# Two-layer hybrid decoder trunk: mixers placed between projection tiles, and retention's rotation moved to VectorE

## The chip, the cores and the metric

One core of one Trainium2 chip runs the whole program. The time is device microseconds of one execution, the median of three runs of the kernel before. All arithmetic is fp32. The engines are named as in the profile: PE is TensorE, DVE is VectorE, ACT is ScalarE, POOL is GpSimd and SP is SyncE, which here issues most transfers.

## What is computed

Two layers (DEPTH = 2) over 544 rows: 512 prompt positions and 8 samples of 4 new positions. D is 1024; every head has 64 channels, and there are 4 heads in retention and 4 in attention. Per layer:

```
h = x @ w_in        # 11 blocks of 256 columns: ret q,k,v,gate | dil q,k,v | conv in (2) | sgu u,v (2)
q_r, k_r = rotary(rq, rk, 64, 1e4);  ro, state = retention(q_r, k_r, rv, s0)     # chunks of 128
y_ret = layer_norm(ro) * silu(rg)
q_b, k_b = rotary(sq, sk, first 16 of 64 dims, 5e5)
y_swa = dilated_attention(q_b, k_b, sv, cached k, cached v)   # (128,1), (512,4), (2048,16), softmax combined
y_conv = silu(layer_norm(causal_depthwise_conv31(val * sigmoid(gate))))
u, v = gelu(sgu_in);  y_sgu = u * (lower_triangular(W) @ layer_norm(v) + b)
x = layer_norm(alpha * x + concat(y_ret, y_swa, y_conv, y_sgu) @ w_out)
x = layer_norm(alpha * x + moe(x))   # 4 groups, best group, best 2 of its 8 SwiGLU experts, 32 experts in all
```

The new states, keys, values and conv rows are outputs too. Each expert has three matrices of 2 MB.

## The kernel before

The kernel is written by hand, one instruction stream per engine. The order of every stream is the order of the code; engines meet through counted semaphores: `E.need(name, n)` waits, `E.done(ins, name)` counts. `E.link` makes an engine wait for its own last result. All of it is `trunk_program`.

A layer goes like this. TensorE turns x (five row tiles: four of 128 rows and one of the 32 sample rows) into `xT`. Then come the projections in chunks: a chunk is one block of 256 columns, whose weights (1 MB) SyncE loads into one of three ring buffers, times the five tiles. `chunk` issues a chunk's tiles; ScalarE's `proj_out` empties each from PSUM into `h` with the activation that belongs to the block. Blocks stand in the order VAL, GATE (conv input), U, V (sgu), RG, RQ, RK, RV (retention), SQ, SK, SV (attention). PSUM has eight banks; projection tiles go round five of them.

While chunks run, the other engines work on blocks that are out. GpSimd multiplies VAL by GATE ("glu"); VectorE normalises V (`group_norm`), copies the conv context and runs 62 taps over 784 columns (L1099 to L1113, two halves of the channels); GpSimd rotates RQ and RK ("rot_r") and SQ and SK ("rot_s") with `rotate`, four small operations per row tile and two large ones per block. In layer 0 GpSimd also issues 22 stores that clear the experts' scratch rows, ahead of "glu".

After the last chunk nothing wide is left: TensorE turns q and k of retention and of attention (`qk_tr`, eight groups), runs retention over four chunks (`ret_scores`, `ret_products`, L650 to L667), the sample's retention, and then attention. Attention is 16 units (4 row tiles times 4 heads). Unit u has scores (`att_scores`), VectorE's mask, maximum and negation (`attend`), ScalarE's exponential, the transposed probabilities (L787), their copy, the values (`att_values`) and VectorE's scaled rows (`att_rows`). The samples' cached keys and values, 16 transfers of 640 KB through four buffers, are taken between units in pairs (`cached_key_scores`, `sample_values`). GpSimd works on retention's norm meanwhile. Then the four mixers' results are turned (`turn_rows` over `mix`), four output chunks follow, x1 is normalised and stored, and the router makes tables of which expert serves which rows: a long chain of small VectorE operations, for which TensorE waits three times.

The experts run in turns over three lanes. SyncE reloads a lane's w1 and w3 as soon as the lane's product has been made, and w2 after the second product. The first three experts are loaded while the output projection runs.

```
                for t in range(TILES):
                    E.need("x1", t + 1)
...
                def load_hidden(q, turn):
                    row, new = item_at(q, turn)
                    sp.wait_ge(sem(f"h_ps{q}"), sp.snap(lo + turn))
```

## Time and profile before

| | |
|---|---|
| median of 3 runs | 1935.23 us (1932.53 to 1937.45) |
| the profiled execution | 1938.98 us |
| its span, first to last instruction | 1936.9 us |
| TensorE busy | 1472.9 us (76%) |
| VectorE, ScalarE, GpSimd busy | 544.6, 208.8, 398.8 us |
| mean granted TensorE clock | 0.854 |
| transfers | 532.60 MB, 275 GB/s on the mean |

The granted clock is the share of full speed that TensorE was given; it has two levels here, 0.5 and 1.0, and a number between them is a mean over both. The busy time of TensorE counts instructions in flight and so says little of how near to its peak the engine works. In the tables of stretches each row is one stretch of time in us from the span's start. In the timeline an f32 matmul of the code is two records, so a 128-row tile of a chunk (eight matmuls) is x16.

### The profile page before, as it was taken

How to read it: one execution, taken by the hardware profiler on the slowest of the kernel's cores; microseconds unless marked ns; L12 is line 12 of the kernel's file. 1: busy time of each engine (PE TensorE's matmuls, PEld its weight loads, DVE VectorE, ACT ScalarE, POOL GpSimd, SP SyncE). 2: the span in 40 equal slices, each digit the busy share in tenths (PEclk: the TensorE clock that was granted, in tenths of full speed). 3: DMA queues.
4: the chain of work that ended last, by engine and by line, in shares of the span. 5: the costliest groups of instructions: out<-in, count | busy, mean ns of one | idle time of the engine just before them, and what ended most of it. 6: DMA issues, size and time to landing. Idle time of an engine off the chain costs nothing. (4 is left out here: it accounts for less than half of the span.)

```text
span 1936.9 us, 40042 instructions
## 1 busy us (share of the span) xinstructions
PE 1472.9 (76%) x16276; PEld 1012.2 (52%) x16276; DVE 544.6 (28%) x1215; ACT 208.8 (11%) x579; POOL 398.8 (21%) x533
## 2 busy tenths in 40 slices
PE   8998899949567576767499988995766758566990
PEld 7887647835334333434488874684433424333550
DVE  0395352541000000000609735236100101000116
ACT  2111030001000000000121112201000000000010
POOL 3149230111001011100311943001211101110113
PEclk9999589969788888879699977896878878887995
DMA  8711041949999999999531102265899999999824
GB/s 341 280 66 58 1 159 64 364 173 359 428 425 382 425 426 425 384 425 386 194 135 66 44 36 109 92 256 225 333 427 425 380 427 424 426 425 425 349 89 142
DMA packets 77409, 532.60 MB, mean 275 GB/s; under 512 B 14430, under 2 KB 31770, under 8 KB 48538
## 3 DMA queue, kind: packets, MB, share of 16 engines
q1 hardware_dynamic: 45466, 482.00, 60.4%
q0 software_dynamic: 11136, 35.40, 5.0%
q10 hardware_dynamic: 20736, 14.18, 2.3%
q8 instruction: 53, 0.87, 0.2%
q14 instruction: 18, 0.15, 0.0%
HBM read 772.37 MB, written 35.98 MB: 417 GB/s over the span
## 5 line engine op out<-in xcount | busy, mean ns | idle before, releaser
L871 PE MATMUL ps<-arena,xT 128*32 128x256 f32 x6912 | 477.8, 437 | 252.1 <-DMA arena<-in_w 250.5
L871 PEld LDWEIGHTS ps<-arena,xT 128*32 128x32 f32 x6912 | 274.9, 126 | 444.7 <-issue 352.9
L542 PE MATMUL ps<-arena,xT 128*128 128x256 f32 x1920 | 424.9, 382 | 0.9 <-issue 0.9
L542 PEld LDWEIGHTS ps<-arena,xT 128*128 128x128 f32 x1920 | 363.9, 191 | 51.5 <-issue 1.0
L1496 DVE COPY xT<-ps 128x128 f32<-128x128 f32 x108 | 31.5, 291 | 907.2 <-PE ps L880 907.2
L889 PE MATMUL ps<-arena,xT 128*32 128x256 f32 x3456 | 212.2, 386 | 34.0 <-DVE xT L1496 22.4
L1674 POOL COPY xT<-xT 128x1 int32 x108 | 19.7, 182 | 805.8 <-PE ps L861 805.8
L889 PEld LDWEIGHTS ps<-arena,xT 128*32 128x32 f32 x3456 | 108.7, 110 | 110.2 <-issue 27.2
L1676 POOL DMA_INDIRECT xT<-x1d,xT x108 | 105.0, 972 | 53.1 <-POOL xT L1674 49.6
L1106 DVE SCALAR_TENSOR_TENSOR arena<-arena 128x784 f32<-128x784 f32 x120 | 113.7, 1029 | 0.0
L1017 ACT ACTIVATE xT<-ps 128x128 f32<-128x128 f32 x108 | 30.0, 278 | 668.7 <-PE ps L871 668.7
L1593 POOL TENSOR_TENSOR arena<-arena,const 128x128 f32<-128x128 f32 (+1 forms) x40 | 68.8, 1719 | 73.9 <-ACT arena L956 73.6
L1022 ACT COPY xT<-ps 128x256 f32<-128x256 f32 x108 | 40.2, 373 | 293.2 <-PE ps L889 289.6
L519 PE MATMUL ps<-const,arena 128*128 128x128 f32 (+1 forms) x240 | 37.8, 311 | 43.0 <-DVE arena L1283 32.8
L953 ACT ACTIVATE arena<-ps 128x256 f32<-128x256 f32 x88 | 33.8, 384 | 273.9 <-PE ps L542 273.9
L519 PEld LDWEIGHTS ps<-const,arena 128*128 128x128 f32 (+1 forms) x240 | 30.5, 167 | 49.6 <-DVE arena L1283 34.4
L1658 POOL TENSOR_TENSOR mv<-mv,halfc 128x1 f32<-128x1 f32 (+1 forms) x10 | 13.3, 1329 | 204.9 <-DVE mv L1307 204.9
L1492 DVE COPY xT<-ps 128x256 f32<-128x256 f32 x114 | 48.4, 425 | 24.5 <-PE ps L861 24.5
L861 PE MATMUL ps<-const,xT 128*128 128x128 f32 x228 | 44.4, 277 | 10.6 <-DMA xT<-x1d,xT 9.5
L940 ACT COPY xT<-ps 128x512 f32<-128x512 f32 (+1 forms) x50 | 24.8, 523 | 189.6 <-PE ps L519 189.4
L1060 DVE TENSOR_REDUCE pstat<-arena 128x20 f32<-128x1280 f32 (+1 forms) x4 | 5.9, 1486 | 124.1 <-ACT arena L956 124.1
L880 PEld LDWEIGHTS ps<-const,xT 128*128 128x128 f32 x108 | 14.9, 138 | 44.5 <-issue 44.5
(244 smaller groups left out, 1223.1 us busy)
## 6 DMA issues: line engine op xcount, KB each, us to landing
arena<-in_w SPq DMA_DIRECT2D x324, 2048.0 KB
arena<-in_w_proj SPq DMA_DIRECT2D x30, 1024.0 KB, 5.0
arena<-in_kv SPq DMA_DIRECT2D x32, 640.0 KB, 5.1
yd<-xT ACTq DMA_DIRECT2D x432, 32.0 KB
yd<-arena POOLq DMA_DIRECT2D x22, 512.0 KB, 18.6
rowpar<-in_rowpar SPq DMA_DIRECT2D x2, 2708.0 KB, 17.2
x1d<-arena SPq DMA_DIRECT2D x8, 512.0 KB, 14.6
arena<-x1d SPq DMA_DIRECT2D x8, 512.0 KB, 6.7
```

The costliest lines, as they stand in the source:

```text
L519: ins = pe.transpose(ps[g][:, j * 128:j * 128 + n], source(t, 4 * g + j), ident[0:n, 0:n])
L542: ins = pe.matmul(bank[0:n, 0:CW], xT[:, k, 128 * t:128 * t + n], ring[slot(c)][:, k, :], start=(k == 0), stop=(k == KT - 1))
L861: ins = pe.transpose(TOKENS[:, b * 128:(b + 1) * 128], xg[q][:, b * 128:(b + 1) * 128], ident)
L871: ins = pe.matmul(HB[q][r, 0:256], xgT[q][:, k % 2, BLK * (k // 2):BLK * (k // 2 + 1)], w13[q][:, :, k, 128 * j:128 * (j + 1)], start=(k = ...
L889: ins = pe.matmul(YB[q][r, 0:256], hT[q][:, BLK * c:BLK * (c + 1)], w2[q][:, c, 256 * t:256 * (t + 1)], start=(c == 0), stop=(c == 3), til ...
L953: ins = act.activation(h[0:n, c, t, :], bank[0:n, 0:CW], func.get(c, ACT.Copy))
L1022: act.copy(yo[q], YB[q][:, 0:256]).then_inc(sem(f"y_out{q}"), 1)
L1106: ins = dve.scalar_tensor_tensor(out=acc[:, cb, :], in0=src, scalar=cw[:, cb * TAPS + j:cb * TAPS + j + 1], in1=acc[:, cb, :], op0=ALU.mul ...
L1492: dve.tensor_copy(xgT[q], TOKENS[:, 0:256].rearrange("p (b m) -> p b m", b=2)).then_inc(sem(f"xgT{q}"), 1)
L1496: dve.tensor_copy(hT[q], HIDDEN[:, 0:128]).then_inc(sem(f"hT{q}"), 1)
L1593: pool.tensor_tensor(t1[:, t], a[:, t], sb_, ALU.mult)
L1676: pool.indirect_dma_start(out=xg[q], out_offset=None, in_=x1q, in_offset=bass.IndirectOffsetOnAxis(ap=gidx[q], axis=0))\
```

## The change

The blocks are projected in another order: VAL, GATE, SQ, SK, SV, RQ, RK, V, RV, U, RG. Attention starts as soon as SQ, SK and SV are out, and its units stand between the tiles of RQ, RK and V; retention's chunks stand between those of RV and U; the mixers' results are turned between the tiles of RG. The projection now goes round two PSUM banks, ps[2] and ps[3], so that a tile waits for the tile two before it to be emptied; the other banks are the mixers'.

Work changes engines. GpSimd no longer rotates. VectorE rotates SQ and SK behind tap 26, and RQ and RK between attention's units 10 and 11 and 12 and 13, with six operations per block. The taps are cut: 38 ahead of attention, 24 between units 0 to 8 (`TAPS_AT`). VectorE also takes k's decay and retention's norm from GpSimd. ScalarE takes the building of QB (the samples' queries, eight small copies) from GpSimd and the conv rows' copies from VectorE. V's GELU is made in one operation after its chunk. GpSimd keeps the powers, the expanded values and the products of "glu".

Turned q and k no longer lie in `xT` but where x is (`sT`, `rT`, and the fourth kv buffer too). So x is loaded again before the output projection, in layer 1 from a copy in memory (`x2d`) that SyncE stores at the start of the layer. The ring has two buffers after the first three chunks. Caches are used four at a time. In the router, `run_idle` issues matmuls whose result nobody reads, where TensorE waits for VectorE.

```diff
-VAL, GATE, U, V, RG, RQ, RK, RV, SQ, SK, SV = range(NCH)
+VAL, GATE, SQ, SK, SV, RQ, RK, V, RV, U, RG = range(NCH)
+TAPS_AT = (38, 41, 44, 47, 50, 53, 54, 57, 59, 62)
...
+                if L:
+                    for t in range(TILES):
+                        sp.wait_ge(sem("x2"), (L - 1) * TILES + t + 1)
+                        sp.dma_start(x2d[128 * t:128 * t + ROWS[t], :], x[0:ROWS[t], t, :]).then_inc(sem("x_saved"), 16)
...
+                ring_load(7)
+                for i in range(2 * NKV, 3 * NKV):
+                    kv_load(i)
+                ring_load(8)
+                for i in range(3 * NKV, 4 * NKV):
+                    kv_load(i)
+                ring_load(9)
+                ring_load(10)
...
+                def tile(c, t):
+                    if t == 0:
+                        pe.wait_ge(sem(f"ring{slot(c)}"), filled(c, L))
+                    j = serial(c, t, True)
+                    if j >= 2:
+                        E.need("proj_out", j - 1)
+                    E.done(weigh(ps[2 + j % 2], c, t), "proj")
...
+                E.need("s_act", 4)
+                E.need("proj_out", (SV + 1) * TILES)
+                att_scores(0)
+                for u in range(16):
+                    if u < 15:
+                        att_scores(u + 1)
+                    if u > 10:
+                        E.need("conv_out", u - 10)
+                    if u:
+                        tile(RQ + (u - 1) // TILES, (u - 1) % TILES)
+                    if 10 <= u < 15:
+                        turn_conv(u - 10, RQ * TILES + u - 1)
+                    att_turn(u)
+                    if u:
+                        att_values(u - 1)
+                    if u == 1:
+                        new_key_scores()
+                        cached_key_scores(range(0, NKV))
+                    if u == 3:
+                        cached_key_scores(range(NKV, NB))
...
+                for n in range(4):
+                    E.need("ret_a", n + 1)
+                    if n < 3:
+                        ret_scores(n + 1)
+                    if n:
+                        E.need("ret_upd", n)
+                    ret_products(n)
+                    ret_rows(n)
+                    tile((RV, RV, U, U)[n], (3, 4, 0, 1)[n])
...
+                for t in range(2, TILES):
+                    turn_mix(t - 2)
+                    tile(RG, t)
...
+                    for k in range(n):
+                        pe.matmul(HIDDEN[:, 0:256], ident, ones2, start=True, stop=True)
...
+                    dve.tensor_tensor(t1, a, si, ALU.mult)
+                    dve.tensor_tensor(t2, b, si, ALU.mult)
+                    dve.tensor_tensor(a, a, co, ALU.mult)
+                    E.link(dve.tensor_tensor(b, b, co, ALU.mult))
+                    dve.tensor_tensor(a, a, t2, ALU.subtract)
+                    return dve.tensor_tensor(b, b, t1, ALU.add)
...
+                    if u < 9:
+                        taps(TAPS_AT[u], TAPS_AT[u + 1])
```

TensorE in the midst of attention, before: the end of unit 3 and unit 4, whose scores, transposes and values follow each other directly (L703 scores, L787 transposes, L731 cached keys, L770 values).

```order
L703 MATMUL ps<-xT 128x256 [waits att_m]
L787 MATMUL ps<-const,arena 128x128 [waits att_pT,att_p]
L787 MATMUL ps<-const,arena 128x128
L731 MATMUL ps<-arena 32x512 [waits kv1,kv0]
L731 MATMUL ps<-arena 32x512
L731 MATMUL ps<-arena 32x128 x2
L731 MATMUL ps<-arena 32x512 x2
L731 MATMUL ps<-arena 32x128 x2
L770 MATMUL ps<-arena 128x64 [waits att_y,att_pT]
```

The same place now (L642 scores, L556 a projection tile, L652 transposes, L660 values):

```order
L642 MATMUL ps<-arena 128x256 [waits att_m]
L556 MATMUL ps<-arena,xT 128x256 [waits proj_out]
L556 MATMUL ps<-arena,xT 128x256 x7
L652 MATMUL ps<-const,arena 128x128 [waits att_y,att_pT,att_p]
L652 MATMUL ps<-const,arena 128x128
L660 MATMUL ps<-arena 128x64 [waits att_pT]
```

A tile of eight wide matmuls now stands between a unit's scores and its transposes, with a wait for ScalarE's emptying of its bank; the wait for VectorE's rows (att_y) moved from the values to the transposes.

VectorE in one unit, before (L1226 inverse, L1205 to L1208 mask, maximum and negation, L1232 rows):

```order
L1226 RECIPROCAL small<-small 128x1 [waits att_p]
L1205 SCALAR_TENSOR_TENSOR arena<-ps,const 128x256 [waits att_t,att_s,dve_chain]
L1207 TENSOR_REDUCE small<-arena 128x1 [waits dve_chain]
L1208 TENSOR_SCALAR small<-small 128x1 [waits dve_chain]
L1232 TENSOR_SCALAR arena<-ps,small 128x64 [waits att_o]
```

And now, with taps (L1231) ahead of the rows (L1283):

```order
L1278 RECIPROCAL small<-small 128x1 [waits att_p]
L1271 SCALAR_TENSOR_TENSOR arena<-ps,const 128x256 [waits att_t,att_s,dve_chain]
L1273 TENSOR_REDUCE small<-arena 128x1 [waits dve_chain]
L1274 TENSOR_SCALAR small<-small 128x1 [waits dve_chain]
L1231 SCALAR_TENSOR_TENSOR arena<-arena 128x784 x2
L1231 SCALAR_TENSOR_TENSOR arena<-arena 128x784 [waits dve_chain]
L1283 TENSOR_SCALAR arena<-ps,small 128x64 [waits att_o,dve_chain]
```

Three taps stand in the unit between the negated maximum and the rows of the unit before.

TensorE in the router, now (L914 to L916 counts and places, L923 onehot products, L929 which; L908 is `run_idle`):

```order
L908 MATMUL ps<-const 128x256 x18
L914 MATMUL ps<-xT,const 128x32 [waits member]
L915 MATMUL ps<-xT,const 128x160
L916 MATMUL ps<-xT,const 128x160
L908 MATMUL ps<-const 128x256 x28
L923 MATMUL ps<-xT 128x120 [waits onehot]
L923 MATMUL ps<-xT 128x120 x9
L908 MATMUL ps<-const 128x256 x4
L929 MATMUL ps<-const,xT 1x40 [waits which]
```

The three groups of L908 are new and wait for nothing; the others stand as before.

## Rows read from the trace of the kernel before

**Rows 1.** Table of stretches: TensorE, weight loads, VectorE, ScalarE, GpSimd; clock, transfers
```profile
5.00:187.00 182.00, 177.85 (x1484) 153.26 (x1484) 90.31 (x113) 35.57 (x98) 85.33 (x106) 1.00 0.48 183
187.00:236.00 49.00, 42.49 (x272) 32.27 (x272) 13.39 (x42) 6.34 (x13) 11.51 (x29) 0.60 0.10 36
236.00:302.00 66.00, 58.13 (x328) 31.77 (x326) 32.12 (x94) 18.85 (x53) 16.30 (x6) 0.83 0.41 147
...
414.00:426.00 12.00, 7.63 (x77) 4.23 (x75) 2.61 (x11) 1.28 (x1) 4.17 (x5) 0.68 0.15 46
...
428.00:850.00 422.00, 293.07 (x4267) 166.28 (x4259) 36.96 (x132) 27.95 (x86) 52.54 (x91) 0.85 0.98 407
```

**Rows 2.** TensorE's timeline, projection: start, length, line, tiles [idle before <-releaser]
```profile
73.35 14.08 PE L542 MATMUL ps<-arena,xT 128*128 128x256 f32 x64
87.36 1.10 PE L547 MATMUL ps<-arena,xT 128*32 128x64 f32 x64
...
90.14 14.08 PE L542 MATMUL ps<-arena,xT 128*128 128x256 f32 x64
...
310.54 14.05 PE L542 MATMUL ps<-arena,xT 128*128 128x256 f32 x64 [0.43 <-issue]
```

**Rows 3.** TensorE's timeline, attention's units 4 and 13 with cached keys and values
```profile
246.20 2.35 PE L731 MATMUL ps<-arena 128*32 128x512 f32 x16
...
248.84 0.70 PE L703 MATMUL ps<-xT 64*128 64x256 f32 x2
...
286.44 1.12 PE L703 MATMUL ps<-xT 64*128 64x512 f32 x2
287.49 0.66 PE L787 MATMUL ps<-const,arena 128*128 128x128 f32 x4
288.08 2.35 PE L758 MATMUL ps<-arena 128*32 128x256 f32 x20
290.36 0.62 PE L760 MATMUL ps<-arena 32*32 32x256 f32 x4
290.91 1.10 PE L770 MATMUL ps<-arena 128*128 128x64 f32 x8
```

**Rows 4.** TensorE's timeline, retention's rows stage
```profile
207.56 0.69 PE L657 MATMUL ps<-arena 128*128 128x64 f32 x2
```

**Rows 5.** GpSimd's timeline: glu, the rotation's first operation, the building of QB
```profile
49.83 2.88 POOL L1573 TENSOR_TENSOR arena<-arena 128x1280 f32<-128x1280 f32 x1
...
121.40 27.75 POOL L1593 TENSOR_TENSOR arena<-arena,const 128x128 f32<-128x128 f32 x1 [36.75 <-ACT arena L956]
...
204.36 1.97 POOL L1638 COPY arena<-xT 64x16 f32<-64x16 f32 x8
```

**Rows 6.** VectorE's timeline: a pass of V's norm, the taps
```profile
76.26 1.49 DVE L1062 TENSOR_TENSOR arena<-arena,pstat 128x1280 f32<-128x1280 f32 x1
...
92.00 56.83 DVE L1106 SCALAR_TENSOR_TENSOR arena<-arena 128x784 f32<-128x784 f32 x60
```

**Rows 7.** ScalarE's timeline: its first table load and what follows
```profile
6.21 1.28 ACT L940 ACT_TABLE_LOAD   x1 [6.21 <-PE ps L519]
7.50 1.07 ACT L940 COPY xT<-ps 128x512 f32<-128x512 f32 x2
```

**Rows 8.** Table of stretches of 4 us, columns as in rows 1
```profile
200.00:204.00 4.00, 3.77 (x18) 3.55 (x18) 0.90 (x4) 0.00 (x0) 3.92 (x5) 0.50 0.00 0
...
264.00:268.00 4.00, 2.31 (x11) 1.44 (x9) 3.72 (x14) 2.12 (x6) 3.92 (x2) 0.59 0.12 50
276.00:280.00 4.00, 4.00 (x25) 1.81 (x27) 1.53 (x3) 1.29 (x3) 0.00 (x0) 0.70 0.00 0
```

**Rows 9.** TensorE's timeline, router (onehot products) and the first two experts' products
```profile
410.26 4.62 PE L843 MATMUL ps<-xT 128*128 128x120 f32 x20 [9.89 <-DVE xT L1459]
...
420.31 6.04 PE L871 MATMUL ps<-arena,xT 128*32 128x256 f32 x64 [1.05 <-DVE xT L1492]
...
427.61 3.66 PE L871 MATMUL ps<-arena,xT 128*32 128x256 f32 x64
```

More of the change, by code:

```diff
@@ L564, in _ @@
+                tile(SQ, 0)
+                tile(SQ, 1)
                 E.need("glu", 1)
@@ new lines, in _, with ret_scores @@
+                E.need("smp_rows", 1)
+                E.need("smp_y", 1)
+                turn_pair(RQ, RK, "r_tr", lambda k: (("r_act", "r_dve")[k % 2], k // 2 + 1))
+                tile(RV, 1)
+                def ret_scores(n):
+                    for hd in range(NH):
+                        hp, hh = hd // 2, hd % 2
+                        ins = pe.matmul(ps[4 + hh][:, hp * 128:(hp + 1) * 128], rT[half(hh), 2 + hp, n * 128:(n + 1) * 128],
+                                        rT[half(hh), hp, n * 128:(n + 1) * 128], start=True, stop=True)
+                    E.done(ins, "ret_s")
@@ new lines, in _ @@
+                E.need("vexp", 1)
+                for hd in range(NH):
+                    hp, hh = hd // 2, hd % 2
+                    ins = pe.matmul(ps[4 + hp][half(hh), :], h[0:NS, RK, 4, hd * HD:(hd + 1) * HD],
+                                    vexp[:, hd, :, :].rearrange("p b e -> p (b e)"), start=True, stop=True)
+                E.done(ins, "smp_o")
+                tile(U, 3)
+                tile(U, 4)
+                E.need("sgu_vn", 1)
+                E.need("sgu_w", 1)
+                wT = CP("sgu_wT").rearrange("p (g t) -> p g t", g=4)
@@ L1098, in _, with taps @@
                 cw, cbias = CP("conv_w"), CP("conv_b")
-                for j in range(TAPS):
-                    for cb in range(2):
+                def taps(first, last):
+                    for k in range(first, last):
+                        j, cb = k // 2, k % 2
                         src = ctxb[:, cb, j:j + ACCW]
@@ new lines, in _ @@
+                for hp in range(2):
+                    ins = dve.scalar_tensor_tensor(out=s0[:, hp, :], in0=s0[:, hp, :], scalar=C("c_decay_s")[:, hp:hp + 1],
+                                                   in1=ps[4 + hp][:, :], op0=ALU.mult, op1=ALU.add)
+                E.done(ins, "smp_upd")
+                centre(last, NH, HD, last_stat)
+                spread(last, NH, HD, last_stat)
+                E.link(along(sv, RP("sgu_ln_g"), ALU.mult))
+                E.done(along(sv, RP("sgu_ln_b"), ALU.add), "sgu_vn")
```

992 lines of the change are left out of this document (508 added, 484 removed).

## The prediction, made before the changed kernel ran

> **What bounds the kernel now.** I read the table of stretches first, since the page's shares average over unlike stages. It shows a layer in four pieces [rows 1]. In 5 to 187 TensorE is busy 177.85 of 182 us: eleven projection chunks. In 187 to 302 (retention, then attention) it counts as busy for 100 of 115 us, but at a granted clock of 0.60 and 0.83. Then come the transposes of the mixers' results, and from 310.5 the output projection [rows 2]. From 428 on the transfers of expert weights keep their engines 0.98 busy: that piece is as long as its bytes, and only its start can move. So the path to the start of a layer's weight stream is TensorE's own order, and the question is how long TensorE needs for it when light and wide work are mixed. VectorE is busy 90.31 + 13.39 + 32.12 us in 5 to 302 [rows 1]; it is not the bound. Layer 1 repeats all this.
>
> The timeline gives the units. A chunk is 14.01 us for four 128-row tiles (3.50 each) and 1.03 for the 32-row tile [rows 2]. At full clock, each from its start to the next row's: a score takes 0.63 us with 256 keys and 1.05 with 512, so 0.41 and 0.84 (estimated) with 128 and 384; turning the probabilities 0.2 to 0.59 and values 0.27 to 1.04 by keys, of which the last are shown; a pair of caches 2.28, and with values 0.55 more [rows 3]. Of retention the trace has only the lower clock: 0.62 us per pair of records in its rows stage [rows 4].
>
> **The change part by part.** First the path of layer 0 up to the first output-projection tile, now at 310.5.
>
> (a) Five chunks, x's transposes and the conv context are there as before: 90.1 us [rows 2]. New: the context transposes now come after chunk 2's second tile (50.4), but GpSimd has the gate's product only at 52.7, because it clears the experts' scratch rows first [rows 5]: +2.4, in layer 0 alone (no clearing in layer 1). Then attention's q and k are turned here, paced by four ScalarE copies of 0.54 [rows 7] with some 0.1 of handoff each: +3.9. The rotation that gates them is VectorE's now, 12 operations of 160 elements at some 0.33, behind tap 26 of 62. Taps start at 55 and take 0.947 each [rows 6], so 26 end at 79, when k's chunk is out, and the rotation ends at 83, before TensorE asks (85): no wait. Sum 96.4.
>
> (b) Start of attention. The first score waits for ScalarE to empty chunk SV (1.1 us, estimated), and the first exponential for eight small copies that now build QB on ScalarE (1.97 on GpSimd [rows 5], taken 2.2), a table load of 1.28 that stands ahead of the wait, and itself, about 0.6. From the last SV tile to the first turned probabilities: 5.2 us, in which TensorE works 0.8. A table load's end is followed by a copy at once: it starts at 6.21, and the copy at 7.50 [rows 7]. The page ScalarE: Activation LUTs of the Trainium skill (section What ACT_TABLE_LOAD costs) gives 2.66 us per switch, a drain included. By that the sum would be 1.4 us worse here in each layer; that row doesn't agree with it.
>
> (c) The attention loop, 16 units with 15 tiles of RQ, RK and V set between: scores 10.9, turning 6, values 9, cached keys and values 20.4, other sample work and conv's transposes 3.7; tiles 12 x 3.50 + 3 x 1.03 = 45.1; sum 95.1, and 3 for handoffs that the mix may uncover: 98.1. VectorE per unit: two passes over up to 512 elements at 1.16 ns (1.49 us for 1280 [rows 6]) with the small operations 1 to 2, three taps 2.84: 4 to 4.7, against TensorE's 4.6 to 6.3. Only units 5, 7, 10 and 12 have more (a rotation is 6 x 0.77 = 4.7); those meet a TensorE unit of equal length. GpSimd no longer rotates: the first operation of that, issued while VectorE ran taps, stood 27.75 us [rows 5]. Its three passes for retention's norm become VectorE's, 1.49 or less each.
>
> (d) Retention with RV and U between. Tiles 30.1; last unit's values 1; transposes 4.5, with GELU of V and its table load ahead of their copies; scores and products 4.4, rows 7.2, sample part 8.5. These last 20.1 us are what the trace has at the lower clock (0.62 per pair [rows 4], 34 in all) taken at about half, as that level is 1.2 against 2.4 GHz. VectorE has two normalisations beside the masks (some 16 operations of up to 1.49), and its last one, V's, ends about 2.5 us after TensorE's last U tile; with two shorter waits on ret_upd 4.5. Sum 60.2.
>
> (e) sgu 2.6 as now, chunk RG 15.05, four turned tiles of 1.04 between, 0.5 of waits, the fifth turned tile 1: 23.3.
>
> Sum 96.4 + 5.2 + 98.1 + 60.2 + 23.3 = 283.2, against 310.5: 27.3 us less in layer 0, 29.7 in layer 1, if the clock stays up. What follows (output projection, x1, router) is as before.
>
> **The clock.** It doesn't stay up. In 200 to 204 TensorE is busy 3.77 of 4 us and gets 0.50; in 264 to 268, busy 2.31 of 4, it falls; it comes back in 276 to 280, under the cached values [rows 8]. The first expert product after a cold stretch takes 6.04 where the next takes 3.66 [rows 9]. So small matmuls with gaps cost the clock, and a piece of wide work pays some 2 us to get it back. Stretch (b) costs one such fall: 2.5. Attention's stretches between tiles are 1.3 to 2.6 us: none. In (d) they are 3 to 5 us, with the 32-row tile between two of them: I take 8, on the lower side of 0 to 24.5 (34 - 20.1 = 14, and six tiles half at the lower clock, 6 x 1.75), since every tile there is wide work and the 34 had none. 10.5 per layer: 16.8 and 19.2 remain, 36 together.
>
> **Idle matmuls** (18, 28 and 4 of 128x256, 0.44 each at full clock, from 3.50 for a tile's eight) fill TensorE's waits in the router. 28 of them are 12.3 us, longer than the 9.89 they stand in [rows 9], and the first four or five run at the lower clock: VectorE's chain goes some 0.8 us later. In return the first expert's product takes 3.66 instead of 6.04, and the weight transfers, 0.15 busy in 414 to 426 [rows 1], go on when it is done. Net 1.5 gained per layer (bounds: 3.5 gained, 2 lost).
>
> SyncE: x is loaded a second time in each layer, 2.1 MB, 5 us at the stream's 407 GB/s [rows 1], beside TensorE's work (in layer 1 it is also stored first). Ring and kv transfers stand behind waits for tiles some units earlier; the tightest is kv 12 to 15 behind ring 8, issued after unit 10's tile, 9 us of bytes for unit 12, 10 to 12 us later. Cost if that cover is gone: 3, inside the 3 of (c). In layer 1 the parameters follow the save, 1 to 2 us later, with the gate's chunk still running.
>
> Sum: 36 + 3 = 39. The profiled execution's own time is 1938.98 (span 1936.9), 3.75 above the median 1935.23; 1938.98 - 39 = 1900.0, and by the median 1896.2. I predict 1897.
>
> **Rivals.**
> 1. Full clock throughout: 27.3 + 29.7 + 3 = 60, time 1875. For it: a wide tile every 4 to 9 us. Against: (b) leaves TensorE idle for 4.4 of 5.2 us, more than 264 to 268, where the clock fell. 0.12.
> 2. Retention stays at the lower clock: 24.5 instead of 8 per layer, +33, time 1930, about no change. For it: 187 to 236 has 0.60 on the mean though busy. Against: no tile stood there. 0.08.
> 3. The engines chain: a unit ends only when VectorE's rows of the unit before are out, and taps lie ahead of these. If each of 16 units is 0.6 us late, +10 per layer, 1917. 0.10.
> 4. Slower: light work between tiles pulls the clock down all through attention too. Each of 24 full tiles runs half at the lower level, 24 x 1.75 = 42; attention's 50 us of light work nearly double, +42; retention +14: 98 against a gain of 27, 71 lost per layer, time about 2075. It decides from 28 us per layer, so when more than a quarter of this comes. For it: the fall in 264 to 268, in the midst of attention. Against: 236 to 302 kept 0.83 on the mean with nothing as wide as a tile in it. 0.06.
>
> **How the numbers follow.** Forecast (1880 to 1912) 0.64, rivals as above. The low end is rival 1 with the idle matmuls near their better bound, 1872; the high end takes in rival 3 and most of the way to rival 2, 1924; outside lie rival 4, the worse half of 2 and a little of each end. 0.3% of this kernel is 5.8 us, about what a measurement can tell from no change. Faster by more: forecast, 1, 3 and half of 2, 0.90. Within: half of rival 2, 0.04. Slower: 0.06.
>
> **What would show it.** Right: first output-projection tile near 294; granted clock 1.00 from unit 1 to unit 15, a fall at the start of attention and one or two in retention; expert products starting 18 us earlier in layer 0. Wrong: VectorE busy without gaps while TensorE waits on its rows (3); stretches at 0.50 over whole tiles (2, 4); waits on kv or ring transfers; router matmuls later than the idle ones allow by more than 1 us.

## The result, and the profile after

The changed kernel takes 1859.5 us (median of 4, 1858.4 to 1860.8) against 1936.3 for the kernel before (median of 4): ratio 0.9607, 95% interval 0.9590 to 0.9623. That is 76.8 us less, where 39 were predicted, and the time lies 12 us below the low end of the range. The profiled execution has a span of 1857.0 us, 79.9 less than the 1936.9 of before; the traces are compared by these spans.

The table of stretches of the changed kernel, columns as in [rows 1]. The stretches are the steps of the prediction: (a) up to SV's last tile, (b) the start of attention, (c) its loop, (d) retention, (e) up to the first output-projection tile; then the same for layer 1.

```profile
5.00:98.50 93.50, 88.91 (x710) 76.14 (x710) 40.20 (x54) 21.01 (x53) 16.77 (x27) 0.96 0.76 297
98.50:103.30 4.80, 0.74 (x9) 0.47 (x5) 2.78 (x8) 4.15 (x15) 0.00 (x0) 1.00 0.62 222
103.30:189.30 86.00, 84.56 (x740) 64.85 (x740) 57.63 (x119) 24.62 (x80) 0.00 (x0) 0.98 0.36 132
189.30:252.00 62.70, 60.65 (x486) 48.73 (x485) 42.51 (x73) 8.48 (x20) 17.37 (x8) 0.89 0.19 67
252.00:273.30 21.30, 21.30 (x187) 18.38 (x177) 8.92 (x20) 7.50 (x18) 0.00 (x0) 1.00 0.22 86
...
1001.90:1088.60 86.70, 85.92 (x741) 65.84 (x740) 57.33 (x120) 24.66 (x80) 0.00 (x0) 0.96 0.35 131
1088.60:1149.80 61.20, 59.15 (x486) 47.28 (x485) 42.39 (x73) 8.44 (x20) 16.29 (x8) 0.92 0.20 68
```

Retention and attention stood at 0.60 and 0.83 in [rows 1]; with the tiles between them they have 0.89 and 0.98, and TensorE is busy in 84.56 of the loop's 86.0 us. The whole gain is in these stretches. TensorE's timeline of the changed kernel has the marks (start, length, line, tiles, idle time before and what ended it):

```profile
273.29 3.72 PE L556 MATMUL ps<-arena,xT 128*128 128x256 f32 x16
...
383.44 5.32 PE L952 MATMUL ps<-arena,xT 128*32 128x256 f32 x64 [0.96 <-DVE xT L1675]
...
904.34 1.97 PE L534 MATMUL ps<-const,arena 128*128 128x128 f32 x8 [23.36 <-DVE arena L1464]
...
1171.05 3.72 PE L556 MATMUL ps<-arena,xT 128*128 128x256 f32 x16
```

The first output-projection tile came at 310.54 in layer 0 [rows 2] and comes at 273.29: 37.25 us earlier. In layer 1 it comes 266.7 us after the layer's first transposes, where the trace of before has 309.3 (939.86 and 1249.19): 42.6 us. Together 79.9, the whole difference of the spans. What follows the two marks moves along: from the first output tile to the first expert's product it is 110.2 us (109.8 before), and the rest, with the weight stream, is as long as it was, within 2 us either way (from layer 0's mark to layer 1's transposes 631.1 for 629.3, behind layer 1's mark 686.0 for 687.7).

### The profile page after: what moved, and what is told of

The parts are those of the page before. It is cut to its first block, busy times and chain, and to the rows that moved or that the text cites. A ratio compares the mean times of both kernels' runs of the same rounds, so it can differ in the third digit from the quotient of the medians.

```text
span 1857.0 us, 40385 instructions
## 1 busy us (share of the span) xinstructions
PE 1448.6 (78%) x16476; PEld 1014.9 (55%) x16476; DVE 572.4 (31%) x1257; ACT 218.0 (12%) x615; POOL 240.3 (13%) x323
## 4 chain that ended last, share of the span: by engine, by line
PE 50%; DMA 39%; DVE 5%; SPq 2%; issue 2%; POOL 1%; ACT 1%; ACTq 0%; DVEq 0%; POOLq 0%
DMA arena<-in_w 36%; PE ps L556 20%; PE ps L952 13%; PE ps L970 3%; PE ps L908 2%; PE ps L561 1%; DVE arena L1711 1%; PE ps L642 1%; DMA arena<-in_ret_state 1%; DVE arena L1461 1%; PE ps L534 1%; DMA arena<-in_kv 1%; PE ps L899 1%; DVE bn L1455 1%; PE ps L660 1%
## 5 line engine op out<-in xcount | busy, mean ns | idle before, releaser
L556 PE MATMUL ps<-arena,xT 128*128 128x256 f32 x1920 | 450.2, 393 | 0.4 <-ACT arena L1033 0.4
L556 PEld LDWEIGHTS ps<-arena,xT 128*128 128x128 f32 x1920 | 371.2, 197 | 68.7 <-issue 15.1
L1231 DVE SCALAR_TENSOR_TENSOR arena<-arena 128x784 f32<-128x784 f32 x120 | 115.3, 1028 | 0.0
L534 PE MATMUL ps<-const,arena 128*128 128x128 f32 (+1 forms) x240 | 35.7, 300 | 39.6 <-DVE arena L1464 32.4
L1746 POOL TENSOR_TENSOR rstat<-rstat,halfc 128x5 f32<-128x5 f32 (+2 forms) x6 | 14.9, 2482 | 333.3 <-DVE rstat L1193 333.3
L908 PE MATMUL ps<-const 128*128 128x256 f32 x200 | 46.0, 388 | 0.0
L908 PEld LDWEIGHTS ps<-const 128*128 128x128 f32 x200 | 38.6, 195 | 5.6
```

What stands on the lines that cost most here:

```text
L534: ins = pe.transpose(ps[g][:, j * 128:j * 128 + n], source(t, 4 * g + j), ident[0:n, 0:n])
L556: ins = pe.matmul(bank[0:n, 0:CW], xT[:, k, 128 * t:128 * t + n], ring[slot(c)][:, k, :], start=(k == 0), stop=(k == KT - 1))
L908: pe.matmul(HIDDEN[:, 0:256], ident, ones2, start=True, stop=True)
L1231: ins = dve.scalar_tensor_tensor(out=acc[:, cb, :], in0=src, scalar=cw[:, cb * TAPS + j:cb * TAPS + j + 1], in1=acc[:, cb, :], op0=ALU.mul ...
```

## Where the 41 us that I missed are

By the prediction's own steps, layer 0, in us:

| step | predicted | measured | difference |
|---|---|---|---|
| (a) to SV's last tile | 96.4 | 98.5 | +2.1 |
| (b) start of attention, with its fall of the clock | 5.2 + 2.5 | 4.8 (the slow tile counts in c) | -2.9 |
| (c) loop | 98.1 | 86.0 | -12.1 |
| (d) retention, with the clock | 60.2 + 8 | 62.7 | -5.5 |
| (e) | 23.3 | 21.3 | -2.0 |
| first output tile | 293.7 | 273.3 | -20.4 |

Step (c) is where most went. Its 15 tiles take 47.3 us (one of them, at 103.91, 5.21 long where 3.72 is usual), one wait for a cache 1.44, so everything else 37.3, where I had 53. The caches stand out. TensorE's timeline of the changed kernel, a batch of cached keys and a batch of values (L690 and L717 with L719):

```profile
122.72 2.36 PE L690 MATMUL ps<-arena 128*32 128x512 f32 x32 [1.44 <-DMA arena<-in_kv]
...
153.39 2.37 PE L717 MATMUL ps<-arena 128*32 128x256 f32 x40
155.69 0.63 PE L719 MATMUL ps<-arena 32*32 32x256 f32 x8
```

These are 32 and 48 records for four caches. In [rows 3] two caches, 16 and 24 records, took the same 2.35 and 2.35 + 0.62. I had priced eight pairs, 20.4 us; the four batches take 10.3. I had written "caches are used four at a time" in my own account of the change and then costed it as a change of order only. The diff also turns `CACHES` from (0, 2, 1, 3, 4, 6, 5, 7) to (0, 2, 4, 6, 1, 3, 5, 7): cache b goes to output partitions 32 (b // 2) and on, so a batch now lies on four different groups of 32. The rows of before already had half of it: one cache's keys are 2 x 640 columns, which by the tiles' price (2048 columns in 3.50) would take 2.19 us (estimated), and a pair, on two groups, took 2.28 from its start to the next row's. The experiments below ask whether the groups are the cause.

## The experiments

Each set of runs has its own runs of before beside it on the same chip. Their medians were 1935.6 (by_pairs, before_four, pool_rot, no_idle), 1936.3 (ret_apart, att_apart, clears_later, early_scores) and 1929.3 (same_groups, ret_moved, both, all4), so I compare ratios; 0.001 is 1.9 us. The changed kernel was not run again with them: a difference to it takes both intervals, and below some 5 us it shows nothing. A trace is one execution, and for by_pairs, pool_rot, same_groups, ret_moved, both and all4 it is the slowest of its set; "by the traces" below carries that.

**Caches by pairs, waits left as they are.**

```diff
-                    for hp in range(2):
+                    for pair, hp in [(p, q) for p in (batch[0:2], batch[2:4]) for q in range(2)]:
...
-                            for i in batch:
+                            for i in pair:
...
-                    for k in range(6):
-                        for i in batch:
+                    for pair, k in [(p, q) for p in (batch[0:2], batch[2:4]) for q in range(6)]:
+                        for i in pair:
```

> Changed kernel (1859.5), but the cached keys and values of a batch of four go through TensorE as two pairs, one behind the other, as before the change; waits, transfers and places stay those of the fours. Theory A (four caches on four different groups of 32 output partitions run beside each other, so that four take the time of two): before, a pair took 2.35 us of keys and 2.35 + 0.62 of values; now four take 2.36 and 2.37 + 0.63. Undone, that is 2 x 2.3 + 2 x 2.9 = 10.4 us more per layer, less up to 1.4 of waits for cache transfers that then lie hidden: 1878 to 1880. Rival B (the loop is shorter for another reason: fewer handoffs, a better clock): within 3 us of 1859.5.

Measured 0.9657 (0.9635 to 0.9679), +9.7 us, half of what I expected. By the traces the first output tiles come 6.8 and 7.5 us later, 14.3 in all, which the two intervals (+4 to +15) still hold. TensorE's timeline of this kernel shows why it is less than 19.

```profile
122.77 3.46 PE L690 MATMUL ps<-arena 128*32 128x512 f32 x32 [0.37 <-DMA arena<-in_kv]
...
154.54 2.35 PE L717 MATMUL ps<-arena 128*32 128x256 f32 x20
156.82 0.62 PE L719 MATMUL ps<-arena 32*32 32x256 f32 x4
157.37 2.35 PE L717 MATMUL ps<-arena 128*32 128x256 f32 x20
```

The values doubled, as theory A says. The keys went from 2.36 to 3.46 only. My reading: the second pair's first matmuls are on other partitions than the first pair's last, so they still ran beside each other. (The values' pairs change groups in the same way and don't overlap; between them stand the four records of 32 rows, L719, and no run takes these away.) The next run tests the reading for the keys.

**The same, in the cache order of before.** That takes this overlap away.

```diff
-CACHES = (0, 2, 4, 6, 1, 3, 5, 7)
+CACHES = (0, 2, 1, 3, 4, 6, 5, 7)
```

> Changed kernel, caches of a batch as two pairs as in by_pairs, but in the order of before (0, 2, 1, 3, 4, 6, 5, 7), so that the second pair lies on the same two groups of 32 output partitions as the first and can't run beside its end. In by_pairs the values took 2.9 more per batch but the keys only 0.8 and 1.1, since the second pair's first matmuls stood on other groups. Theory A (it is the groups): now the keys take 4.6 per batch too, some 10 per layer in all, less up to 1.4 of cache waits hidden: 1876 to 1879. Rival B (the keys are bound by something else, such as loading 512-wide rows, and don't overlap at all): as by_pairs, 1868 to 1870.

Measured 0.9707 (0.9680 to 0.9733), +19 us on the changed kernel (+13 to +25 with both intervals), with the keys of a batch at 4.50:

```profile
124.96 4.50 PE L690 MATMUL ps<-arena 128*32 128x512 f32 x32
```

Theory A holds in its size too: the batches' matmuls alone are 9.8 us longer per layer, less the cache waits of 1.44 and 0.79 (layer 1) that are gone, 17.4 in all, so the partition groups are worth about 19 of the 77 us. The list of cache numbers alone, with everything else equal, moved keys from 3.46 to 4.50. That is 2.1 us per layer, 4.2 in both; the ratios of the two kernels differ by 9.6 (3 to 16 with both intervals), of which more than the keys' share isn't shown.

**The fours alone, in the kernel before.** Batches at units 0, 5, 11 and 14, nothing interleaved.

```diff
-                    if u in (0, 2, 4, 6):
-                        cached_key_scores(u)
+                    if u in (0, 5):
+                        cached_key_scores(4 * (u > 0))
...
-                    if u in (11, 12, 13, 14):
-                        sample_values(2 * (u - 11))
+                    if u in (11, 14):
+                        sample_values(4 * (u > 11))
```

> Kernel before (1936), with the one part that takes caches in fours, on four groups of 32 partitions, at units 0, 5, 11 and 14; nothing is interleaved. Theory A: 10.4 us less per layer in TensorE's busy time, of which some comes back as waits, for caches at unit 14 (2.6 MB to load again behind unit 11) and for the units' own chain of exponentials, which the pairs covered: 1915 to 1922. Rival B: within 3 us of 1936, either since four don't run beside each other or since TensorE only waits where it worked.

Measured 0.9983 (0.9967 to 1.0000): 3 us, not 14 to 21. In its trace, the stretch of attention (columns as in [rows 1]) and the last batch of values on TensorE's timeline:

```profile
236.00:302.00 66.00, 54.74 (x336) 32.98 (x335) 30.21 (x94) 19.43 (x54) 16.30 (x6) 0.71 0.40 147
```
```profile
285.27 4.49 PE L758 MATMUL ps<-arena 128*32 128x256 f32 x40 [2.33 <-DMA arena<-in_kv]
```

The same cut of matmul time came back two ways: waits of 1.62 (keys, at 252.28) and 2.33 (values) for caches, and a granted clock of 0.71 where the pairs had 0.83 [rows 1], at which three of the four batches ran 4.49 or 4.50 long instead of 2.37. I had expected waits only. So the 19 us belong to the fours and to the tiles around them together.

**The tiles out of attention.** All 15 tiles of RQ, RK and V, and all taps, ahead of the units; V's weights are loaded earlier so that they are there.

```diff
-TAPS_AT = (38, 41, 44, 47, 50, 53, 54, 57, 59, 62)
+TAPS_AT = (62,) * 10
...
-                    if u:
-                        tile(RQ + (u - 1) // TILES, (u - 1) % TILES)
...
+                for j in range(3 * TILES):
+                    tile(RQ + j // TILES, j % TILES)
                 E.need("s_act", 4)
```

> Changed kernel, with the 15 tiles of RQ, RK and V issued ahead of attention and all 62 taps too, so that the units follow each other directly; caches still in fours. Theory A: the units alone took 66 us before (0.83) with 10 us more of cache matmuls, while now loop and tiles take 86, of which 45.1 are tiles. Apart, 45.1 + 56 to 60: 15 to 19 us more per layer, 1890 to 1898. Rival B (the gain lies in the caches and in the engines, not in the mixing): within 5 us of 1859.5.

Measured 0.9868 (0.9841 to 0.9894), +50 us, more than the 30 to 38 that theory A gave. Two rows of its TensorE timeline tell what is in it:

```profile
162.62 4.50 PE L689 MATMUL ps<-arena 128*32 128x512 f32 x32 [7.78 <-DMA arena<-in_kv]
...
196.72 0.87 PE L651 MATMUL ps<-const,arena 128*128 128x128 f32 x3 [3.69 <-DVE arena L1282]
```

The wait for the second batch of keys grew from 1.44 to 7.78, since units without tiles reach it sooner and V's weights are now loaded ahead of these caches (which of the two weighs more isn't shown); the longest other wait is for VectorE's rows behind its rotation, which stand uncovered; and part of the batches and units run at the lower clock (0.87 for a unit's three transposes, 0.49 with tiles around). The layer's traces part the two: from SV's last tile to RV's first it is 26 us more than in the changed kernel, 13 of them idle time of TensorE (18.5 against 5.5) and 13 the same matmuls at a lower clock.

**The tiles out of retention.** RV's last four and U's five in one run ahead of it.

```diff
-                tile(RV, 1)
+                for t in range(1, TILES):
+                    tile(RV, t)
+                for t in range(TILES):
+                    tile(U, t)
...
-                    tile((RV, RV, U, U)[n], (3, 4, 0, 1)[n])
```

> Changed kernel, with the nine tiles of RV and U that stood between retention's pieces issued in one run ahead of them. Theory A (wide tiles between the pieces hold TensorE's clock and cover the waits for VectorE and ScalarE): this stage took 62.7 us in layer 0 at 0.89; with 26.9 us of tiles at full clock, 5 for turning q and k, and retention alone as before the change (some 39 us from its first scores to 236 at 0.60), it is 71 to 75: 8 to 12 us more per layer, 1876 to 1884. Rival B (mixing does nothing in this stage, as the clock falls there anyway): within 4 us of 1859.5.

Measured 0.9850 (0.9833 to 0.9866), +47 us, again more than expected. Rows of its timeline on TensorE:

```profile
232.21 1.22 PE L783 MATMUL ps<-arena 64*128 64x128 f32 x8 [4.75 <-DVE arena L1353]
...
273.69 3.78 PE L851 MATMUL ps<-arena 128*128 128x256 f32 x8 [6.98 <-DVE arena L1198]
...
278.07 7.17 PE L556 MATMUL ps<-arena,xT 128*128 128x256 f32 x32
```

Sgu's matmuls start at 273.69, where the changed kernel has them at 252.05. The norms that came from GpSimd to VectorE and V's norm take VectorE's time; with tiles between the pieces TensorE works meanwhile, without them it waits (4.75 and 6.98 are the longest). My 8 to 12 us per layer took retention to be as long as before the change, when GpSimd made these norms. From RV's first tile to sgu's matmuls it is 85.6 us here and 62.7 in the changed kernel; 17 of these 23 are idle time (19.2 against 2.1) and 6 are slower matmuls, so the cover that the tiles give VectorE is the larger part in this stage. The mixing is worth some 50 us in each stage given the rest of the change, and the two overlap with the fours: the parts don't add up to 77.

**Retention's rotation back on GpSimd.**

```diff
                     if u == 10:
-                        E.need("proj_out", (RQ + 1) * TILES)
-                        E.link(rotate(RQ, 32, "rcos", "rsin", ctx_acc))
+                        pass
...
+                E.need("proj_out", (RQ + 1) * TILES)
+                E.link(rotate(RQ, 32, "rcos", "rsin"))
+                E.need("proj_out", (RK + 1) * TILES)
+                E.done(rotate(RK, 32, "rcos", "rsin"), "rot_r")
```

> Changed kernel, with the rotation of RQ and RK back on GpSimd in the form it had before (four small operations per row tile, two large ones per block). Theory A (the new order is what gains, not the engine of this rotation): RQ is out at 131 in layer 0, the taps end at 148, a block takes GpSimd 12 to 14 us once they are over, so the rotation ends near 176 and TensorE asks at 193: within 2 us of 1859.5. Rival B (GpSimd held by VectorE's operations all through attention, or the power operations behind it late): the turned q and k of retention wait, 5 to 20 us per layer, 1870 to 1900.

Measured 0.9603 (0.9581 to 0.9624), the same as the changed kernel. GpSimd's timeline of this kernel:

```profile
132.49 0.46 POOL L1775 TENSOR_TENSOR arena<-arena,const 128x128 f32<-128x128 f32 x1 [77.87 <-ACT arena L1033]
...
136.20 1.20 POOL L1776 TENSOR_TENSOR arena<-arena,const 128x128 f32<-128x128 f32 x1
...
169.27 1.54 POOL L1781 TENSOR_TENSOR arena<-arena 128x640 f32<-128x640 f32 x1
```

It is done at 170.8, 23 us before TensorE turns q and k (193.66). An operation issued during taps took 1.2 us here, where the one of [rows 5] stood 27.75: then 60 taps ran without a gap, now three at a time. VectorE pays too: its three taps at 135.91 took 3.48 us, in the changed kernel 2.92. The half of the change that its title names second bought nothing that shows, once the rest of the new order is there.

**No idle matmuls.**

```diff
-                    for k in range(n):
+                    for k in range(0):
```

> Changed kernel without the idle matmuls in the router. Theory A (as in my prediction, net gain 1.5 per layer): 1862 to 1863. By the trace of the changed kernel the 28 of them end 1.1 us after the onehot rows were due, the counts behind them run 2.2 us faster at full clock, and the first expert's product takes 5.32 instead of 6.04: 1.5 to 2 per layer, 1862.5 to 1863.5. Rival B (the end of a layer is set by the weight transfers, whose start doesn't depend on this): 1859.5 within 1 us.

Measured 0.9617 (0.9594 to 0.9641), within the noise of the changed kernel; rival B. Its router, and then that of the changed kernel:

```profile
373.37 4.16 PE L923 MATMUL ps<-xT 128*128 128x120 f32 x20 [9.90 <-DVE xT L1642]
...
382.64 5.85 PE L952 MATMUL ps<-arena,xT 128*32 128x256 f32 x64 [0.71 <-DVE xT L1675]
```
```profile
363.89 12.25 PE L908 MATMUL ps<-const 128*128 128x256 f32 x56
375.98 2.39 PE L923 MATMUL ps<-xT 128*128 128x120 f32 x20
```

The router's last logits start at 348.34 without and 349.65 with the idle matmuls; from there the products with the onehot rows begin after 25.0 us without and 26.3 with: the 28 end 1.3 us late. These products then run 1.8 faster, but waits of 0.29, 1.28 and 0.96 let the clock fall again, so that the first expert takes 5.32 (5.85 without) and not 3.66. From the logits to the row behind that product it is 40.1 us without and 39.0 with (layer 1: 39.6 and 38.6): 1.0 gained per layer by the traces, which the ratio (0.0010, 1.9 us) neither shows nor denies.

**Clears behind the gate's product.**

```diff
-                if L == 0:
-                    for k in range(CLEARS):
...
                 E.done(pool.tensor_tensor(h[:, VAL], h[:, VAL], h[:, GATE], ALU.mult), "glu")
+                if L == 0:
+                    for k in range(CLEARS):
```

> Changed kernel, with the 22 stores that clear the experts' scratch rows issued by GpSimd behind the gate's product. Theory A: in layer 0 the wait of 2.58 at 50.3 goes, and the fall of the clock behind it (the tile pair of 9.09 where 7.17 is usual, transposes of 1.97 where 1.04 is usual, 2.8 together): 5 us less, 1854 to 1855. Rival B (the stores, 11 MB, then meet the loads of later weight blocks or of the caches, and a tile waits for its weights): 1859 or above.

Measured 0.9566 (0.9548 to 0.9584), 7 to 8 us less, where 5 were expected; by the span 6.3. The wait of 2.58 and the slow tile behind it are gone, and SV's last tile comes 4.8 us earlier. The first output tile of layer 0 comes 6.5 us earlier: the other 1.8 arose behind the edited place, in where the clock fell. TensorE's timeline, context transposes and the tiles behind them, of the changed kernel and of this one:

```profile
52.91 1.97 PE L596 MATMUL ps<-const,arena 128*128 128x128 f32 x8 [2.58 <-POOL arena L1756]
...
55.26 9.09 PE L556 MATMUL ps<-arena,xT 128*128 128x256 f32 x32
```
```profile
50.71 1.04 PE L596 MATMUL ps<-const,arena 128*128 128x128 f32 x8
...
52.43 7.17 PE L556 MATMUL ps<-arena,xT 128*128 128x256 f32 x32
```

**First scores between SV's tiles.** ScalarE's QB copies move behind the second exponential.

```diff
-TAPS_AT = (38, 41, 44, 47, 50, 53, 54, 57, 59, 62)
+TAPS_AT = (34, 38, 42, 46, 50, 53, 54, 57, 59, 62)
...
+                tile(SV, 2)
                 E.need("s_act", 4)
-                E.need("proj_out", (SV + 1) * TILES)
                 att_scores(0)
+                tile(SV, 3)
+                tile(SV, 4)
```

> Changed kernel, with attention's first scores made behind SV's third tile, their exponential (and its table load) ahead of the emptying of SV's last two tiles, the eight QB copies behind the second exponential, and 34 taps ahead of attention where there were 38. Theory A: the 4.0 us in which TensorE is idle between SV's last tile and the first turned probabilities go, and so does the fall of the clock behind (a tile of 5.21 in layer 0 and 6.38 in layer 1 where 3.72 is usual): 5.5 to 6.5 us less per layer, 1847 to 1849. Rival B (VectorE, with four more taps among the units, ends units late): the gain is given back in the loop, 1856 to 1862.

Measured 0.9540 (0.9508 to 0.9573), 13 us less by the ratio and 9.4 by the medians, where 11 to 13 were expected; by the span 7.8. TensorE's timeline of it, from the first scores on:

```profile
94.74 0.49 PE L639 MATMUL ps<-arena 64*128 64x128 f32 x2
95.16 3.72 PE L556 MATMUL ps<-arena,xT 128*128 128x256 f32 x16
98.81 1.10 PE L561 MATMUL ps<-arena,xT 128*32 128x64 f32 x64
99.84 0.48 PE L639 MATMUL ps<-arena 64*128 64x128 f32 x2
100.26 0.33 PE L649 MATMUL ps<-const,arena 128*128 128x128 f32 x1
100.52 0.48 PE L639 MATMUL ps<-arena 64*128 64x128 f32 x2
100.93 3.72 PE L556 MATMUL ps<-arena,xT 128*128 128x256 f32 x16
```

No idle time, and the first tile of RQ at its full-clock 3.72 (5.21 in the changed kernel). Layer 0's first output tile comes 5.0 us earlier. In layer 1, counted from its first transposes, the loop ends 5.7 us earlier, but the first output tile comes after 268.2 us, where the changed kernel has 266.7: the gain is lost again in retention. One of the losses is a wait ahead of sgu's matmuls, with U's last full tile ahead of it:

```profile
1134.70 3.72 PE L556 MATMUL ps<-arena,xT 128*128 128x256 f32 x16
...
1141.75 2.62 PE L854 MATMUL ps<-arena 128*128 128x256 f32 x8 [2.29 <-DVE arena L1206]
```

The changed kernel has no such wait, but there the same tile took 6.51 (and 6.56 in layer 0). This alternates: of the eight kernels here that keep retention's order (the changed one, by_pairs, same_groups, pool_rot, no_idle, clears_later, this one and both), nine of the sixteen layers traced have this tile slow (6.3 to 6.6) and no wait, and seven have it at 3.72 and a wait of 2.29 or 2.30. VectorE's norm of V ends 6.9 us after the product ahead of this tile (in layer 0 of the changed kernel, of no_idle and of ret_moved), and the full tile and the 32-row tile between cover only 4.7.

**Other places for retention's tiles.**

```diff
-                    tile((RV, RV, U, U)[n], (3, 4, 0, 1)[n])
+                    for t in ((RV, 3), (RV, 4)) if n == 0 else ((U, n - 1),):
+                        tile(*t)
```

> Changed kernel with another placing of the same tiles in retention: RV's last two tiles behind the first piece, U's first three behind the next three pieces, its fourth behind the sample's state product, and RG's first ahead of sgu's matmuls, so that no 32-row tile stands alone between two pieces. Theory A (the clock fell near 216 since only the 32-row tile, 1.1 us, stood between 2.9 and 3 us of 64-column matmuls; a full tile there keeps it up): the fall's 3.3 us (1.64 for 1.10, two groups of 1.2 for 0.7, a tile of 5.41 for 3.72) go in each layer, and RG's tile covers sgu's wait for V's norm: 1852 to 1855. Rival B (the clock falls anyway, a piece later, or VectorE's norms set the end of this stage): 1858 to 1862.

Measured 0.9605 (0.9579 to 0.9632), nothing; rival B. In TensorE's timeline the clock falls in full tiles now, and sgu still waits for VectorE's norm of V:

```profile
216.81 5.36 PE L556 MATMUL ps<-arena,xT 128*128 128x256 f32 x16
...
226.11 5.41 PE L556 MATMUL ps<-arena,xT 128*128 128x256 f32 x16
...
240.46 5.41 PE L556 MATMUL ps<-arena,xT 128*128 128x256 f32 x16
...
256.50 2.62 PE L854 MATMUL ps<-arena 128*128 128x256 f32 x8 [2.29 <-DVE arena L1203]
```

The 32-row tile was not the cause of the fall. In both placings the falls come behind pieces of retention (3 to 4 us of scores, products and rows, most of them 64 columns wide); which property of these pieces the clock answers to stays open. RG's tile could not cover the wait: as U's fourth tile moved ahead of the sample's state product, there is again one full and one 32-row tile between that product and sgu.

**Together.**

> Changed kernel with the clears behind the gate's product and the early first scores together. Alone they gave 7.7 (of which 5 were expected, in layer 0 alone) and 9.4. They lie at different places of TensorE's order, so they add up: 1840 to 1844. Rival (less than the sum: taps start 2.4 us earlier in both, so VectorE has no slack to be shared, or the loads of caches are the next wait): 1846 to 1850.

Clears and early scores: 0.9534 (0.9507 to 0.9562); its median of 1843.0 lies in the expected 1840 to 1844. By the spans of the profiled executions the two add up: 6.3 and 7.8 alone, 13.5 together. By the ratios the pair can't be told from early scores alone.

> As both, with the tiles of ret_moved, and with 25 idle matmuls where there were 28 (they ended 1.1 us after the rows they bridge) and five more ahead of the first expert's product, in the two waits for its tokens. If each does what I think: both's time, less ret_moved's gain (4 to 7), less 2 to 5 for the first product at full clock in both layers (5.32 and 5.35 for 3.66) and the earlier onehot rows: 1829 to 1837. Rival (idle matmuls are worth nothing again, since the weight transfers and not this product set the pace): 1835 to 1840.

```diff
-                run_idle(28)
+                run_idle(25)
...
+                run_idle(3)
                 turn_tokens(0, first + L)
+                run_idle(2)
```

Measured 0.9506 (0.9478 to 0.9534). The median is 1836.1, within both the expected range and its rival's. This is the fastest kernel here, 5% below the kernel before, and its interval lies clear of the changed kernel's. Its TensorE timeline shows the first expert's product at full clock, with idle ones (L909) ahead of it:

```profile
377.76 1.03 PE L909 MATMUL ps<-const 128*128 128x256 f32 x4
378.72 3.66 PE L953 MATMUL ps<-arena,xT 128*32 128x256 f32 x64
```

From the router's last logits (344.42) to the row behind this product it is 37.9 us, against 39.0 in the changed kernel and 40.1 without idle matmuls: the better places give 1.1 us more. Against `both` the gain (0.0028) isn't clear of the noise. The placing of ret_moved did not help in this trace: layer 0's first output tile comes 7.3 us later than in `both`, with three tiles of 5.3 to 5.4 in retention and the wait of 2.29, and the spans differ by 0.6.

## Why the prediction was wrong, point by point

- **What bounds the kernel: right.** The path is TensorE's own order up to the output projection; the two layers' marks hold the whole 79.9 us, and the weight stream moved without changing its length.
- **(a), 96.4: 2.1 too low.** The 2.4 us wait for the gate's product was seen (2.58). That it also costs the clock was not: transposes of 1.97 for 1.04 and a tile pair of 9.09 for 7.17, 2.8 together. Against that, turning attention's q and k took 3.0 and not 3.9. clears_later had SV's last tile 4.8 earlier.
- **(b), 5.2: right** (4.8). Its fall of the clock, 2.5, was right in size as well: the first tile of RQ lost 1.5 in layer 0 and 2.7 in layer 1 (6.38 for 3.72). The table load took 1.28 as in [rows 7], and the exponential behind it began at once. ScalarE's timeline of the changed kernel:

```profile
99.40 1.82 ACT L1068 COPY arena<-arena 64x16 f32<-64x16 f32 x8
101.24 1.28 ACT L1076 ACT_TABLE_LOAD   x1
102.54 0.40 ACT L1076 ACTIVATE arena<-arena,small 128x128 f32<-128x128 f32 x1
```

- **(c), 98.1 against 86.0: the step that failed.** The term "cached keys and values 20.4" was eight times the price of a pair, carried over from the kernel before; it measured 10.3. same_groups and by_pairs show the mechanism: small matmuls on different groups of 32 output partitions run beside each other, four in the time of two. It is 10 us per layer, 20 in all, half of what I missed. The other half has no single step: it is the sum of the differences at the other points here. Of the rest, the 3 us for "handoffs that the mix may uncover" weren't needed: the loop waits once, 1.44, for a cache. Scores, turning, values and the small sample work came out 2.6 below my sum of full-clock prices, and 2.2 went back in the tiles, 1.5 of it in the slow one.
- **(d), 60.2 + 8: 5.5 too high, since a wait and a fall of the clock cover each other.** I gave 4.5 us to waits, 2.5 of them for V's norm behind the last U tile, and 8 to the clock, as a sum. The trace has no such wait: sgu's matmuls follow U's 32-row tile directly (252.05), 0.5 us after VectorE's norm ended at 251.5. But the 2.5 was well seen: where U's last full tile ran at full clock, the wait is 2.30 (early_scores above). In the changed kernel that tile was slow and took the wait's place, so that of the two only one is paid. That the waits for ret_upd didn't come is simply a term too high. TensorE's timeline of the changed kernel:

```profile
251.02 1.10 PE L561 MATMUL ps<-arena,xT 128*32 128x64 f32 x64
252.05 1.99 PE L853 MATMUL ps<-arena 128*128 128x256 f32 x8
```

- **The clock in (d), 8 us: right in size.** 62.7 us at a mean grant of 0.89 lose 0.11 x 62.7 = 6.9, in layer 1 0.08 x 61.2 = 4.9 (estimated, as if every part of the stretch went by the clock). I had it in one or two falls; there are three in layer 0, in 4 us stretches of the changed kernel:

```profile
216.00:220.00 4.00, 4.00 (x80) 3.54 (x70) 3.89 (x8) 0.86 (x4) 0.00 (x0) 0.57 0.34 98
...
224.00:228.00 4.00, 4.00 (x16) 3.31 (x16) 3.75 (x3) 0.18 (x1) 4.00 (x3) 0.70 0.02 4
...
244.00:248.00 4.00, 4.00 (x10) 2.84 (x9) 3.11 (x7) 0.00 (x0) 0.77 (x1) 0.50 0.53 189
```

- **(e): 2.0 too high.** The waits of 0.5 weren't there, and the fifth turned tile comes behind the first output tile.
- **Idle matmuls, 1.5 per layer:** 1.0 by the traces, within the noise by the times; right within what can be told. The clock fell again in the waits behind them, which I hadn't looked at.
- **The rivals.** Rival 1, full clock throughout, gave 1875, and the measured time is below even that, though the clock did fall: what I left out lay in the price of work, not in the clock. Rival 3 (VectorE's taps ahead of rows) didn't come; 57.6 us busy in 86. Rivals 2 and 4 didn't either.
- **The signs I had named.** Right were the clock of 1.00 in attention from its second unit on and the fall at its start; the first output tile near 294 and the first expert 18 us earlier were far off (273.3, and 36.9 earlier). Two signs of being wrong showed, a wait for caches (1.44, covered by my 3) and a stretch at 0.50 over a tile (244 to 248), and a third by a hair, the idle matmuls 1.3 us late where I had allowed 1. None of them pointed at the term that failed, which has no sign in the list.
- **The range** was built from the clock and from waits. No term had an end for "this matmul work itself gets cheaper", so it couldn't hold the result.

Not settled: the +47 and +50 us of the two kernels without mixing hold side effects of their own (a cache wait of 7.78), and although their traces part idle time (17 of 23 and 13 of 26 us in layer 0) from slower matmuls, they don't tell how much of the slower clock the idle time itself brought about. Where the clock falls in retention differs between executions and kernels, which moves single traces by some us. Explained is the difference of the layers: layer 1's gain is 5.4 us larger than layer 0's, as much as the clears' wait (2.6) and the slow matmuls behind it (2.8), which only layer 0 has.

## What to carry to other kernels

When a diff changes which operands share a batch, or only a list of indices that picks where results land, cost the matmuls anew by their partitions. Compare a row's length with its columns at the price of a wide tile: the pair of before, 2.28 where one cache alone would take 2.19 (estimated), already said that two ran beside each other, and asked what four would do. Cutting light work on an engine that then waits buys little (3 us here), while the same cut among wide tiles bought 19; so test a part both in the old and in the new arrangement before calling it small. Don't simply add a wait for another engine to a fall of the clock just ahead of it: here one covered the other. And give every term of a sum an end on the cheap side.

## What the runs showed of the hardware

- Matmuls with 32 output partitions, in fp32: two caches on two groups 2.35 us for the keys, four on four groups 2.36, four on two groups 4.50, and 3.46 when only the boundary between the pairs is on different groups. For the values that boundary gave no overlap (2.35 + 0.62 twice), with records of 32 rows between the pairs.
- GpSimd operations that run against VectorE's taps of two operands took 1.2 instead of 0.45 us when the taps came in threes, and one stood 27.75 when they came without a gap [rows 5]; three taps beside them took VectorE 3.48 us instead of 2.92.
- A wait of 2.6 us of TensorE amid full-clock tiles cost 2.6 and then 2.8 more in slow matmuls behind it; a wait of 1.44 in the loop cost only itself (the tile behind it, at 125.64, took 3.72). It isn't the same each time: behind the router's wait of 2.1 the next transposes took 1.97 in the changed kernel and 1.10 in no_idle.
- The clock can fall with TensorE busy without a gap (216 to 220 at 0.57, 4.00 of 4 us busy), and it did so behind retention's narrow matmuls in both placings of the tiles that were tried.
